# The first block's MLP: block products by a seven-product scheme, block sums on VectorE

## The reference, cut to what matters

```python
def channel_mlp(h, w1, b1, w2, b2):
    return jnp.square(jax.nn.relu(h @ w1 + b1)) @ w2 + b2

def deepnorm_update(x, y, gate, g, b):
    return layer_norm(ALPHA * x + gate * y, g, b)

x_new = deepnorm_update(x_new, channel_mlp(modulate(x_new, sh2, sc2), w1[l], b1[l], w2[l], b2[l]), g2, ln2_g[l], ln2_b[l])
```

## Time and profile before

| | before |
|---|---|
| median of three runs | 4188.57 us |
| the profiled execution | 4196.7 us |
| its span, first to last instruction | 4195.4 us |
| TensorE busy | 3744.7 us (89%) |
| VectorE busy | 1822.5 us (43%) |
| ScalarE busy | 1069.4 us (25%) |
| GpSimd busy | 503.4 us (12%) |
| mean DMA rate | 90 GB/s |
| mean granted clock of TensorE | 0.948 of full speed |

### The profile page before, as it was taken

The page is one execution under the profiler, slowest core; times in us unless marked ns, Lnnn a source line. Parts: engine busy times, 40 slices in busy tenths (PEclk is TensorE's granted clock), DMA queues, the critical chain, the costliest instruction groups (busy, mean ns, idle before and its releaser), DMA issues. The chain is left out here.

```text
span 4195.4 us, 55588 instructions
## 1 busy us (share of the span) xinstructions
PE 3744.7 (89%) x22304; PEld 2203.8 (53%) x22304; DVE 1822.5 (43%) x3869; ACT 1069.4 (25%) x2301; POOL 503.4 (12%) x314
## 2 busy tenths in 40 slices
PE   5999667899999997999987897898899988797898
PEld 4465333344444443655655686444565655686444
DVE  3144565010102011378873653333278874553343
ACT  2221144000001001220113554222230114554322
POOL 0010223000000000002210211110001221211110
PEclk7999879999999998999998998999999999898999
DMA  6332421323441343113321005320213321104310
GB/s 207 131 124 77 138 78 68 123 79 140 146 140 60 130 151 107 47 46 95 100 78 64 26 29 158 102 76 20 65 46 87 109 78 47 41 31 130 130 59 37
DMA packets 218556, 377.64 MB, mean 90 GB/s; under 512 B 30134, under 2 KB 131774, under 8 KB 217302
## 3 DMA queue, kind: packets, MB, share of 16 engines
q1 hardware_dynamic: 214830, 371.15, 26.8%
q10 hardware_dynamic: 3488, 3.08, 0.2%
HBM read 291.50 MB, written 69.08 MB: 86 GB/s over the span
## 5 line engine op out<-in xcount | busy, mean ns | idle before, releaser
L3175 PE MATMUL win_acc<-win_wt,hTl 128*128 128x384 f32 (+3 forms) x3072 | 909.0, 457 | 18.0 <-DMA win_wt<-in_w_in 18.0
L3175 PEld LDWEIGHTS win_acc<-win_wt,hTl 128*128 128x128 f32 x3072 | 561.7, 191 | 359.9 <-DMA win_wt<-in_w_in 18.8
L1543 PE MATMUL mlp_bk<-hTl,mlp_w 128*128 128x512 f32 x1024 | 443.9, 596 | 21.9 <-DMA mlp_scale<-in_norm_g 21.9
L1565 PE MATMUL mlp_bk<-mlp_w,mlp_aT 128*128 128x512 f32 x1024 | 440.3, 592 | 2.3 <-ACT mlp_aT L1448 1.6
L2247 DVE TENSOR_SCALAR_CACHE_REDUCE win_rl<-d_sc,win_mid 128x384 f32<-128x384 f32 (+5 forms) x384 | 363.1, 945 | 41.1 <-DVE win_mid L2255 29.2
L1543 PEld LDWEIGHTS mlp_bk<-hTl,mlp_w 128*128 128x128 f32 x1024 | 195.7, 191 | 267.5 <-issue 245.2
L1565 PEld LDWEIGHTS mlp_bk<-mlp_w,mlp_aT 128*128 128x128 f32 x1024 | 194.2, 190 | 246.3 <-issue 246.3
L1350 DVE TENSOR_SCALAR mlp_r<-mlp_bk,mlp_b 128x512 f32<-128x512 f32 x64 | 48.1, 751 | 494.4 <-PE mlp_bk L1543 484.3
L3017 PE MATMUL tail_wo<-tail_w_out,tail_yT 128*128 128x512 f32 x512 | 228.9, 601 | 9.3 <-issue 9.3
L440 PE MATMUL zin_acc<-zin_wt,hTl 128*128 128x512 f32 (+2 forms) x640 | 229.2, 513 | 0.0
L3028 PE MATMUL tail_wg<-tail_w_gate,tail_xT 128*128 128x512 f32 x512 | 225.3, 594 | 1.0 <-DVE tail_xT L2858 1.0
(11 more groups left out here) (448 smaller groups left out, 5598.3 us busy)
## 6 DMA issues: line engine op xcount, KB each, us to landing
mlp_w<-in_w SPq DMA_DIRECT2D x48, 2048.0 KB, 7.9
win_wt<-in_w_in SPq DMA_DIRECT2D x18, 1536.0 KB, 9.2
s_z<-win_ot SPq DMA_DIRECT2D x14, 1536.0 KB, 7.0
mid_w_out<-in_w_ada SPq DMA_DIRECT2D x8, 2048.0 KB
hTl<-s_z SPq DMA_DIRECT2D x16, 832.0 KB, 4.6
win_zp<-win_ot SPq DMA_DIRECT2D x8, 1344.0 KB
front_w<-in_w_ada SPq DMA_DIRECT2D x4, 2048.0 KB, 15.7
zin_wt<-in_w_in SPq DMA_DIRECT2D x4, 2048.0 KB, 9.8
```

The costliest lines, as they stand in the source:

```text
L1543: mm = pe.matmul(bk[:, 4 * half + f % 2, :], wv[:, k, f * P:(f + 1) * P], hT[:, k, half * HT * P:(half + 1) * HT * P], start=k == 0, stop= ...
L1565: mm = pe.matmul(bk[:, bank(n0 + t_) + q, :], aT[:, 4 * c + f, group(2 * pair + t_)], wv[:, f, q * COL:(q + 1) * COL], start=c == 0 and f ...
L3175: mm = pe.matmul(acc[:, u % RING, 0:w], hT[:, k, t * P:(t + 1) * P], wt[:, i % 2, k, 0:w], start=k == 0, stop=k == KC - 1)
```

## The change

Each of the two products is seen as a product of two by two blocks and made from seven block products and fifteen block sums (the Winograd form of Strassen's scheme) instead of eight products.

- Up: the blocks are halves of the hidden units, of the features and of the 512 tokens. One "round" q makes 128 hidden units of either half: seven products of 4 matmuls with 256 columns (`product`). There are 16 rounds in each half.
- Down: the blocks are halves of the hidden units, the two token tiles of a pair, and the two column halves. A round takes one group of 128 hidden units from either half: seven matmuls of 512 columns, each accumulated over the 16 rounds of a pass in a bank of its own.
- VectorE makes the sums of the operands: four per up round (512 elements each), eight per down round (four of 512, four of 128; `weight_sums`), and four of 1024 elements per half for the tokens (`token_sums`, one before the first round, the other after round 22 of 96, as rounds are numbered through the stage). Sums of the results: five operations per up round (`combine_up`) and seven per down pass (`combine_pass`).
- Bias and relu move from VectorE to ScalarE, which also copies one bank per up round and two per down pass out of PSUM (`copies`, `pass_copies`).
- The weights have two buffers instead of three. A chunk is still 2 MB (two rounds) but two transfers of 1 MB; the rows of the `w1` chunks are 1 KB instead of 2 KB. Chunk i is issued when all rounds of chunk i-2 are done.
- The streams no longer begin with the wait for `const_in`; TensorE waits for weights, `token_sums` and the first `weight_sums`.
- `residual` begins after `combine_pass`: the gate's product now reads `t`, 1024 elements, not PSUM. For tiles 0 and 1 all of it moves to the down pass of the second pair of the first half (beginning at round 32), as for 4 and 5 in the second half; 2 and 3 stay in the up pass. Transposes are taken in two halves (`TURN_AT`), two rounds apart in down passes.

On VectorE, round n of the loop does `combine_up(n - 1)` if it was an up round, then `weight_sums(n + 1)`, then what belongs to the norms, then `combine_pass` in a pass's last round. The core of the diff:

```diff
+    rounds = []
+    for half in range(2):
+        rounds += [("up", half, 0, q) for q in range(HF)]
+        rounds += [("down", half, pair, q) for pair in range(2) for q in range(HF)]
+    B1, B2, B3, B4, B5, B6, B7 = 0, 5, 3, 6, 2, 1, 4
+    TURN = 7
...
-        w = ph.sb("w", [P, 3, KC * COL])
+        w = ph.sb("w", [P, 2, KC * COL])
+        sums = ph.sb("sums", [P, 2, 3, COL])
+        asums = ph.sb("asums", [P, 2, 3, P])
+        tsums = ph.sb("tsums", [P, 3, KC // 2, QT])
+        x15 = ph.sb("x15", [P, 2, COL])
+        v = ph.sb("v", [P, 2, COL])
...
+                    if i >= 2:
+                        sp.wait_ge(done, START + 2 * (i - 1))
                     if kind == "up":
-                        sp.dma_start(w[:, i % 3, :].rearrange("p (k n) -> p k n", k=KC), w1[:, :, c * COL:(c + 1) * COL]).then_inc(w_in[i % 3], DMA)
+                        for s in range(2):
+                            sp.dma_start(w[:, i % 2, :].rearrange("p (k s n) -> p k s n", k=KC, s=2)[:, :, s, :],
+                                         w1[:, :, s * HF * P + q * P:s * HF * P + (q + 2) * P]).then_inc(w_in[i % 2], DMA)
                     else:
-                        sp.dma_start(w[:, i % 3, :].rearrange("p (f n) -> p f n", f=4), w2[:, 4 * c:4 * c + 4, :]).then_inc(w_in[i % 3], DMA)
+                        for s in range(2):
+                            sp.dma_start(w[:, i % 2, :].rearrange("p (s f n) -> p s f n", s=2, f=2)[:, s, :, :],
+                                         w2[:, s * HF + q:s * HF + q + 2, :]).then_inc(w_in[i % 2], DMA)
...
+                stores = [first_of("down", 0, 1) // 2 + 5, first_of("up", 1) // 2 + 4, first_of("down", 1, 1) // 2 + 5]
...
+                def weight_sums(n):
...
+                    dve.wait_ge(w_in[n // 2 % 2], START + (n // 4 + 1) * 2 * DMA)
+                    if n >= 2:
+                        dve.wait_ge(done, START + n - 1)
+                    if rounds[n][0] == "up":
...
+                        k = d(dve.tensor_tensor(s1, a21, a22, ALU.add))
+                        dve.wait_ge(dstep, START + k)
+                        k = d(dve.tensor_tensor(s2, s1, a11, ALU.subtract))
+                        dve.wait_ge(dstep, START + k)
+                        dve.tensor_tensor(a21, a11, a21, ALU.subtract).then_inc(summed, 1)
+                        dve.tensor_tensor(s4, a12, s2, ALU.subtract).then_inc(summed, 1)
+                        return
...
+                    d(dve.tensor_tensor(s1, a21, a22, ALU.add))
+                    k = d(dve.tensor_tensor(t1, b12, b11, ALU.subtract))
+                    dve.wait_ge(dstep, START + k)
+                    d(dve.tensor_tensor(s2, s1, a11, ALU.subtract))
+                    k = d(dve.tensor_tensor(t2, b22, t1, ALU.subtract))
+                    dve.wait_ge(dstep, START + k)
+                    dve.tensor_tensor(a21, a11, a21, ALU.subtract)
+                    dve.tensor_tensor(b12, b22, b12, ALU.subtract).then_inc(summed, 1)
+                    dve.tensor_tensor(s4, a12, s2, ALU.subtract)
+                    dve.tensor_tensor(t4, b21, t2, ALU.subtract).then_inc(summed, 1)
...
+                def combine_up(n):
...
+                    dve.wait_ge(copied, START + u + 1)
+                    dve.wait_ge(part, START + 3 * u + 2)
+                    k = d(dve.tensor_tensor(v[:, 0, :].rearrange("p (a b) -> p a b", a=2), b26.rearrange("p (a b) -> p a b", a=2),
+                                            p1.unsqueeze(1).to_broadcast([P, 2, QT]), ALU.add))
+                    dve.wait_ge(dstep, START + k)
+                    dve.wait_ge(part, START + 3 * u + 3)
+                    k = d(dve.tensor_tensor(v[:, 1, t2], v[:, 0, t2], b74[:, t1], ALU.add))
+                    dve.wait_ge(dstep, START + k)
+                    k = d(dve.tensor_tensor(v[:, 1, t1], v[:, 1, t2], b74[:, t2], ALU.add))
+                    dve.wait_ge(dstep, START + k)
+                    k = d(dve.tensor_tensor(v[:, :, t2], v[:, :, t2], p5.unsqueeze(1).to_broadcast([P, 2, QT]), ALU.add))
+                    dve.wait_ge(dstep, START + k)
+                    dve.wait_ge(done, START + n + 1)
+                    dve.tensor_tensor(v[:, 0, t2], v[:, 0, t2], bk[:, 3, t2 if u % 2 else t1], ALU.add).then_inc(vready, 1)
...
+                def combine_pass(g):
...
+                    dve.wait_ge(pair_made, at + 2)
+                    dve.tensor_tensor(t[:, 0, hi], c1, bk[:, B6, :], ALU.add).then_inc(pair_summed, 1)
...
+                    dve.wait_ge(pair_copied, START + 2 * g + 2)
+                    dve.tensor_tensor(t[:, 0, hi], t[:, 0, hi], c5, ALU.add).then_inc(pair_summed, 1)
+                    dve.wait_ge(pair_made, at + 7)
+                    dve.wait_ge(pair_summed, at + 5)
+                    dve.tensor_tensor(t[:, 0, hi], t[:, 0, hi], bk[:, B3, :], ALU.add).then_inc(pair_summed, 1)
+                    dve.tensor_tensor(t[:, 1, hi], t[:, 1, hi], c5, ALU.add).then_inc(pair_summed, 1)
...
+                    if n and rounds[n - 1][0] == "up":
+                        combine_up(n - 1)
+                    if n + 1 < NR:
+                        weight_sums(n + 1)
...
+                        if k == 0:
+                            first, second = residual(m), residual(m + 1)
+                            next(first, None)
+                        if k == 1:
+                            next(second, None)
+                            next(first, None)
+                        if k == 2:
+                            next(second, None)
+                            next(first, None)
...
+                            next(second, None)
...
+                def copies(n):
...
+                    act.wait_ge(part, START + 3 * u + 1)
+                    act.activation(x15[:, u % 2, :], bk[:, 4 * (u % 2) + 1, :], ACT.Copy).then_inc(copied, 1)
+                def squares_up(n):
...
+                    act.wait_ge(vready, START + u + 1)
...
+                    for j in range(2):
...
+                        ins = act.activation(v[:, j, :], v[:, j, :], ACT.Relu, bias=b1[:, f:f + 1])
...
+                    for j in range(2):
...
+                        ins = act.activation(aT[:, j * HF + q, :], v[:, j, :], ACT.Square)
+                    ins.then_inc(squared, 1)
...
+                def product(out, a, b):
+                    for k in range(KC // 2):
+                        mm = pe.matmul(out, a[:, k, :], b[:, k, :], start=k == 0, stop=k == KC // 2 - 1)
+                    return mm
...
+                def up(n):
...
+                    pe.wait_ge(w_in[n // 2 % 2], START + (n // 4 + 1) * 2 * DMA)
...
+                    pe.wait_ge(summed, START + 2 * n + 1)
+                    product(b26[:, c2], s2, t2)
+                    product(b15[:, c2], s1, t1)
+                    product(b15[:, c1], a11, b11).then_inc(part, 1)
+                    product(b26[:, c1], a12, b21).then_inc(part, 1)
+                    product(b74[:, c1], a21, b12)
+                    product(b74[:, c2], a22, t4).then_inc(part, 1)
+                    pe.wait_ge(summed, START + 2 * n + 2)
...
+                        pe.wait_ge(vready, START + u)
...
+                    product(bk[:, 3, c2 if u % 2 else c1], s4, b22).then_inc(done, 1)
...
+                def down(n):
...
+                    first, final = q == 0, q == HF - 1
...
+                    pe.wait_ge(w_in[n // 2 % 2], START + (n // 4 + 1) * 2 * DMA)
...
+                    m1 = pe.matmul(bk[:, B1, :], a11, b11, start=first, stop=final)
+                    pe.wait_ge(summed, START + 2 * n + 1)
...
+                    m2 = pe.matmul(bk[:, B6, :], s2, t2, start=first, stop=final)
...
+                    m3 = pe.matmul(bk[:, B5, :], s1, t1, start=first, stop=final)
...
+                    m4 = pe.matmul(bk[:, B2, :], a12, b21, start=first, stop=final)
...
+                    m5 = pe.matmul(bk[:, B7, :], a21, b12, start=first, stop=final)
+                    pe.wait_ge(summed, START + 2 * n + 2)
...
+                    m6 = pe.matmul(bk[:, B4, :], a22, t4, start=first, stop=final)
...
+                    m7 = pe.matmul(bk[:, B3, :], s4, b22, start=first, stop=final)
+                    if final:
+                        m1.then_inc(pair_made, 1)
...
+                        m7.then_inc(pair_made, 1)
+                        pe.wait_ge(pair_made, START + 7 * g + 7)
+                        pe.sem_inc(done, 1)
+                    else:
+                        m7.then_inc(done, 1)
```

More of the change, by code:

```diff
@@ L1280, in mlp @@
+        w_sum = lambda n, j: sums[:, n % 2, j, :].rearrange("p (k c) -> p k c", k=KC // 2)
+        TURN_AT = {}
+        for n in range(6):
+            g = n // 2
+            start = first_of("up", 1) if g == 1 else first_of("down", g // 2, 1) if g == 0 else first_of("down", 1, 1)
+            gap = 1 if g == 1 else 2
+            TURN_AT[n] = [start + (3 if g == 1 else 5) + gap * (2 * (n % 2) + h) for h in range(2)]
         with ph.block() as block:
@@ L1343, in s, with d @@
```

(68 more changed lines are left out.)

378 lines of the change are left out of this document (198 added, 180 removed).

## The result

| | median us | runs |
|---|---|---|
| before | 4191.33 | 4 runs, 4187.76 to 4195.99 |
| after | 4082.45 | 4 runs, 4079.42 to 4083.70 |

The ratio is 0.9739 (95% interval 0.9722 to 0.9755), a gain of 108.9 us. Forecast were 4092, with 4076 to 4114 as range: right in sign and inside the range, but the gain is nearer the 110 of rival 1 than the 96 of the forecast, and 4082 lies under the likeliest case's own 4085 to 4100. The MLP alone gave 103.8 us, between the two; the other 5 us come from outside it and are less than the 7 us that the interval leaves open.

The account below looks back on a forecast made before the run. TensorE was taken to bound the MLP almost without holes. Products -107.1, start -8.2, turn waits +16.8, entries +1, clock +5.1, removed waits -6.5 and tail +2.9 sum to -96.0 us, giving 4092 us, range 4076 to 4114.

Parts of the forecast that it names:

- rival 1: Smaller waits in the MLP, by half-speed contention or luck in the order, and no clock fall: -110 us, 4079; chance 0.22.
- the likeliest case: The forecast itself for the whole kernel, 4092 us, given as 4085 to 4100 with chance 0.50.
- The products: Up and down matmuls in the MLP: fewer or shorter instructions at known paces, -52.2 and -54.9, together -107.1 us.
- The start: Before the MLP's first matmul: TensorE starts at about 742.3 instead of 750.51, -8.2 us (between -4 and -9).
- Steady rounds at nothing: Up and down rounds away from the turn: VectorE's sums and the weights stay covered by matmuls, cost 0.
- rival 2: Down chunks: VectorE or weights late in every one, 0.5 us for each of 32: +16, 4109; chance 0.12.
- The tail: From last product to next stage: GpSimd ends 21.3 us behind the last product instead of 18.3, +2.9 us (0 to 5).
- The waits behind the turn: Rounds 32 on and 80 on: TensorE waits for VectorE's sums, partly held by GpSimd; 8.4 us each, +16.8.
- The transposes are placed at least a round behind their input: MLP transposes: the old wait of 2.55 us goes, within the -6.5 us of old waits and clock loss removed.
- The clock: TensorE's clock falls behind some three waits of 2 us and more, 1.7 us each: +5.1 us (0 to 10).
- Rival 4: Down passes: the clock falls as a rule, after a wait in each of 32 chunks: +38 us, 4227; chance 0.03.
- the entries: First rounds of passes behind up passes: the fourth product waits for the last combination, about +1 us.

## Why the prediction was right, and where not

**The products: right.** Waits apart, the stretch fell by 98.6 + 6.9 = 105.5 us (TensorE's gaps in it went from 4.8 to 11.7, the clock's loss is 3.9 in both) against 107.1. Most of the missing 1.6 is an effect of the waits, too, by an estimate: a matmul's recorded length reaches 0.592 - 0.429 = 0.16 us beyond its pace, so a wait costs that much more than its idle time, and there are seven waits more, 1.1 us. A steady up round takes 12.09 us (12.1), a down round 6.01 (6.0). The two experiments with one product more price each part by itself.

**The start: right,** -8.0 for -8.2. VectorE's first sum, released by the landing, starts 9.3 us behind the issue (9.2 reckoned, with the guess of 0.8), and TensorE follows 2.3 us later (2.1).

```profile
727.98 1.01 SPq L1322 DMA_DIRECT2D mlp_w<-in_w  x2
...
737.31 0.69 DVE L1403 TENSOR_TENSOR mlp_sums<-mlp_w 128x512 f32<-128x512 f32 x1 [4.55 <-DMA mlp_w<-in_w]
...
738.77 0.69 DVE L1407 TENSOR_TENSOR mlp_w<-mlp_w 128x512 f32<-128x512 f32 x1
...
739.61 5.83 PE L1679 MATMUL mlp_bk<-mlp_tsums,mlp_sums 128*128 128x256 f32 x16 [13.94 <-DVE mlp_w L1407]
```

**Steady rounds at nothing: right.** No wait in the windows above. A megabyte of weights lands 6.9 us behind its issue, against 7.7 to 8.9 for two in one transfer, so two transfers in place of one made nothing late, and rival 2 is out.

```profile
mlp_w<-in_w SPq DMA_DIRECT2D x96, 1024.0 KB, 6.9
```

The kernels with more sums show the room: two sums more, 1.4 us a round, brought the steady down rounds a single wait, five brought waits to more than half of them. The slack of 0.7 to 1.7 us in the prediction is borne out.

**The tail: right,** +2.8 for +2.9; GpSimd ends 21.1 us behind the last product (21.3 reckoned). The terms that the prediction lists up to GpSimd's start add up to 9.6 us, though, not to its 11.8: the statistics of both tiles (1.6 each) come before it in the trace and are listed once. It began at 11.7.

```profile
1535.41 0.69 DVE L1471 TENSOR_TENSOR mlp_t<-mlp_t,mlp_bk 128x512 f32<-128x512 f32 x1
...
1546.50 2.34 POOL L1366 TENSOR_TENSOR mlp_t<-mlp_t,mlp_rows 128x1024 f32<-128x1024 f32 x1 [79.31 <-ACT mlp_t L1613]
...
1553.63 2.35 POOL L1368 TENSOR_TENSOR mlp_t<-mlp_t,mlp_rows 128x1024 f32<-128x1024 f32 x1
```

**The waits behind the turn: mechanism right, size wrong.** This is the step that failed ("One such stage: 7.2 to 9.6 us, I take 8.4"). The waits for sums were 2.8 us in the first half and 3.0 in the second; with TensorE's wait for its own last product it is 3.2 and 3.3, 6.6 in all for 16.8. The waits for sums in rounds 33, 34 and 35 (0.4, 0.2 and 1.9 reckoned) did not occur, but for 0.18 in round 83, and the two beside GpSimd were 1.15 and 1.67 for 2.0 to 4.4 and 2.65.

VectorE was earlier than the timetable, and the more so the further on. Counted from the end of round 31, the first signal of round 33's sums came at 6.4 us (7.3 reckoned), that of round 35 at 19.8 (21.4), that of round 37 at 35.1 (38.2 with one hold-up by GpSimd ahead of the signal of round 36, and there was one). The combination began before the round's end and was over at 3.6 for 4.5, and a sum that follows on costs 0.60 to 0.61 us for 0.69.

How much is an error at the head of such a chain worth? The kernel with the eighth matmul in down shows it in its first half, where VectorE came 1.6 us earlier into the turn. The changed kernel:

```profile
1031.91 1.10 PE L1728 MATMUL mlp_bk<-mlp_w,mlp_aT 128*128 128x512 f32 x2 [0.41 <-PE mlp_bk L1750]
...
1065.80 0.68 DVE L1422 TENSOR_TENSOR mlp_w<-mlp_w 128x512 f32<-128x512 f32 x1
```

The kernel with the eighth matmul:

```profile
1050.12 1.10 PE L1728 MATMUL mlp_bk<-mlp_w,mlp_aT 128*128 128x512 f32 x2 [0.41 <-PE mlp_bk L1754]
...
1082.43 0.68 DVE L1422 TENSOR_TENSOR mlp_w<-mlp_w 128x512 f32<-128x512 f32 x1
```

From the start of round 32 to round 37's sum it is 33.9 us in the one and 32.3 in the other. The wait of 1.15 went and that of 1.68 stayed, and TensorE came to the second product of round 37 after 33.0 us in place of 34.6. So the waits of a chain add up to how late its last signal is, and 1.6 us at the head count once.

Of the 5.1 us by which a half was charged too much, 1.2 were half of a second hold-up, which came behind the signal; some 3 are VectorE's earliness at round 37; the remaining 1 was paid but is not in the idle time (0.16 us a wait, as above, and waits too short to be listed). That VectorE and GpSimd keep each other out held: no operation ran at half speed, each waited for the whole other one, and without GpSimd's operations the waits went. So the MLP came out between the forecast and rival 1: for a part of rival 1's second reason (shorter waits, and one fall of the clock instead of none), not for its first (half speed). That the 108.9 us lie so near rival 1's 110 is luck, since 5.1 of them come from outside the MLP.

The rule of the Trainium skill (SBUF — State Buffer, SBUF: two separate sides) that such a pair is an exclusive lock agrees with these runs: 2.32 and 2.43 us for sums that take 0.29.

**"The transposes are placed at least a round behind their input": wrong.** The input came a round late, since the reciprocal stood behind a round of sums in VectorE's queue. Cost 2 x 2.32 = 4.6 us; moved a round later, it went. The prediction counted what each step costs VectorE, but not that a step of one tile's chain waits for what is queued ahead of it.

**The clock: too dear,** +5.1 for the new falls less 1.7 for the old one. The loss in the products (the stretches at the lower clock, times the share that it lacks) was 3.9 us before and after, 2.2 of it at the start and 1.7 behind one transpose; it was 5.6 in the second execution of the changed kernel. Rival 4 is out as the loop stands; the kernel with five more sums shows it in a weak form (32.8 us lost to the clock beside 81.4 of waits).

In the MLP this sums up: all waits behind the turn, the transposes' included, 16.8 - 11.2 = 5.6 too dear, the clock 3.4, the entries 0.5, the tail 0.1; the gain in the products 1.6 and at the start 0.2 too large: 96.0 + 7.8 = 103.8. The total is better than its parts, by luck: 10.2 us too much for the sums' waits stand against 4.6 for transposes that nobody had reckoned with.

**What lies outside the MLP.** The medians differ by 108.9, 5.1 more than the MLP. The 2.9 us ahead of it are of stages that the change does not touch. In the next stage (-8.8) the profile of before is the odd one: it took 503.5 us there, and all thirteen profiles with another MLP took 494.2 to 496.8, also that of the kernel with only the start moved (496.4). At one place of it, before has three of VectorE's operations of 6 elements held up by GpSimd, where after has two:

```profile
2088.89 6.66 POOL L3103 TENSOR_TENSOR win_zp<-win_zp,win_ot 128x3072 f32<-128x3072 f32 x1 [39.48 <-DMA win_zp<-s_z]
2089.22 6.36 DVE L2251 COPY_PREDICATED d_lo<-win_ge,win_mid 128x6 f32<-128x6 uint8 x1 [0.24 <-DVE win_lt L2249]
...
2095.72 6.60 DVE L2253 COPY_PREDICATED d_hi<-win_lt,win_mid 128x6 f32<-128x6 uint8 x1
...
2102.38 6.69 POOL L3107 TENSOR_TENSOR win_ot<-win_ot,win_zp 128x3072 f32<-128x3072 f32 x1
2102.56 6.53 DVE L2255 TENSOR_SCALAR win_mid<-win_mid 128x6 f32<-128x6 f32 x1
```

The third hold is 6.5 us, but it is not shown to be the cause: over the whole stage the operations of 6 elements that took over 0.7 us took 50.9 us more than their usual 0.17 before and 49.3 after, since after lost more at other places (5.12 and 4.47 us in place of 2.00 and 3.27 at two of them). The 5.1 us of the medians are within the 7 us of the interval; where they come from, if they are more than scatter, stays open.

**The best version** is the changed kernel with the norms spread: 4071.95 us, ratio 0.9701 to before; with the tail on VectorE as well it is the same within the scatter.

## What to carry to other kernels

Where TensorE is the bound without holes, work taken from it comes out of the time at its pace; read the pace from the trace for each shape, and give the engine that pays for it a budget per round: the same 128 sums cost 5 to 7 us in rounds of 12 us and 22 to 24 in rounds of 6. The losses are where another chain shares that engine with the sums, at the turn of passes, and not in the steady rounds; spread the other chain by one step a round and move its consumers later, before taking any work away. In a chain of leftover waits reckon how late the last signal is, and not wait by wait: 1.6 us at its head took 1.6 us off the whole chain. Small errors of each round's work add up in it to 3 us over five rounds.

## What was not expected of the hardware

- GpSimd holds up even very small operations of VectorE on SBUF: a copy of 6 elements took 6.36 and 6.60 us in place of 0.17 beside a GpSimd operation of 3072 elements (6.7 us), and a one-input operation of 6 elements 6.53. Others are not held: a reciprocal of one element kept its 0.16 us beside GpSimd, the statistics their 1.29 for two, and a TENSOR_TENSOR of 512 elements with an input in PSUM its 0.68.
- The same wait of 2.32 us was followed by 4 us at a mean granted clock of 0.57 in one half and by none in the other, and in another execution of the same kernel by a fall in both.
- VectorE at 67% of a stretch left TensorE without one hole, at 96.8% it left holes of 13.5 us in 100.
